# Modulation units summed by VectorE, modulation as columns, and bias masks shared by two engines

## The reference

```
mod = (silu(c) @ w_mod + b_mod)            # 1024 x 6144, one row; block two: w_ada
sh1, sc1, gt1, sh2, sc2, gt2 = split(mod, 6)
h = layer_norm(x) * (1 + sc1) + sh1
y = hybrid_mixer(h, ...)                   # h @ w_in; convolution, state space part, attention, gates, w_o
x = layer_norm(alpha * x + (1 + gt1) * y)
h = layer_norm(x) * (1 + sc2) + sh2
y = hierarchical_moe(h, ...)               # 16 experts
# block two: latent attention, three banded attentions with
#   bias_table[t5_bucket(pos_k - pos_q)] added to the scores, 16 wider experts
```

## Time and profile before

| | us |
|---|---|
| median of 3 runs | 2214.21 (2212.7 to 2215.25) |
| the profiled execution | 2215.75 |
| its span | 2213.9 |
| TensorE busy | 1644.6 (74%) |
| VectorE busy | 440.2 (20%) |
| ScalarE busy | 287.3 (13%) |
| GpSimd busy | 104.3 (5%) |
| DMA | 670.55 MB, 303 GB/s in the mean |
| granted clock of TensorE | 0.873 |

### The profile page before, as it was taken

The page is one execution under the profiler, slowest core; times in us unless marked ns, Lnnn a source line. Parts: engine busy times, 40 slices in busy tenths (PEclk is TensorE's granted clock), DMA queues, the critical chain, the costliest instruction groups (busy, mean ns, idle before and its releaser), DMA issues.

```text
span 2213.9 us, 19952 instructions
## 1 busy us (share of the span) xinstructions
PE 1644.6 (74%) x8097; PEld 860.0 (39%) x8097; DVE 440.2 (20%) x890; ACT 287.3 (13%) x602; POOL 104.3 (5%) x99
## 2 busy tenths in 40 slices
PE   6899999979998699999998744655464544554444
PEld 2575654444443477687754411311121111211111
DVE  6430542342222322121325300000000000000001
ACT  6211222020000222121223100000000000000000
POOL 7000000000000100111111000000000000000000
PEclk9999999979999799999999777877778766877777
DMA  8899444729998342443452479999999999999995
GB/s 276 293 340 341 178 157 142 295 90 429 426 429 316 128 152 78 166 138 133 137 169 105 200 335 428 428 427 429 427 429 427 428 427 428 427 429 427 428 427 247
DMA packets 116171, 670.55 MB, mean 303 GB/s; under 512 B 8643, under 2 KB 11400, under 8 KB 85360
## 3 DMA queue, kind: packets, MB, share of 16 engines
q1 hardware_dynamic: 111568, 657.50, 73.3%
q0 software_dynamic: 3744, 11.11, 1.7%
q10 hardware_dynamic: 768, 0.64, 0.1%
HBM read 661.88 MB, written 7.34 MB: 302 GB/s over the span
## 4 chain that ended last, share of the span: by engine, by line
PE 61%; DMA 31%; DVE 3%; ACT 2%; issue 2%; SPq 1%; POOL 0%; DVEq 0%; ACTq 0%; POOLq 0%
PE psum L914 13%; PE psum L904 12%; DMA ring<-in_w_up 10%; DMA ring<-in_w_down 10%; PE psum L1403 10%; DMA ring<-in_w_gate 9%; PE psum L1217 5%; PE psum L1247 3%; PE psum L872 2%; PE psum L1187 2%; PE psum L1257 1%; PE psum L1143 1%; SPq L643 1%; PE psum L1340 1%; PE psum L1277 1%
## 5 line engine op out<-in xcount | busy, mean ns | idle before, releaser
L1403 PE MATMUL psum<-work,prob 128*32 128x512 f32 x1024 | 286.5, 724 | 159.0 <-DMA ring<-in_w_up 83.9
L1403 PE MATMUL psum<-ring,prob 128*32 128x512 f32 x1024 | 286.5, 724 | 151.1 <-DMA work<-in_w_up 86.2
L914 PE MATMUL psum<-ring,hT 128*128 128x512 f32 x672 | 303.8, 597 | 4.7 <-ACT hT L177 2.9
L904 PE MATMUL psum<-hT,ring 128*128 128x256 f32 x1152 | 277.2, 385 | 1.6 <-DVE hT L177 1.6
L904 PEld LDWEIGHTS psum<-hT,ring 128*128 128x128 f32 x1152 | 213.7, 193 | 36.3 <-issue 10.6
L1403 PE MATMUL psum<-work,hT 128*32 128x512 f32 x512 | 138.4, 703 | 88.8 <-DMA ring<-in_w_down 88.8
L1403 PE MATMUL psum<-ring,hT 128*32 128x512 f32 x512 | 138.4, 703 | 55.6 <-DMA work<-in_w_down 54.0
L914 PEld LDWEIGHTS psum<-ring,hT 128*128 128x128 f32 x672 | 123.9, 191 | 135.7 <-issue 129.1
L1403 PEld LDWEIGHTS psum<-work,prob 128*32 128x32 f32 x1024 | 70.7, 131 | 261.7 <-issue 261.7
L1403 PEld LDWEIGHTS psum<-ring,prob 128*32 128x32 f32 x1024 | 70.6, 131 | 253.1 <-issue 253.1
L177 ACT ACTIVATE work<-psum 128x512 f32<-128x512 f32 (+2 forms) x99 | 56.0, 566 | 608.3 <-PE psum L1389 236.5
(11 more groups left out here) (322 smaller groups left out, 1581.1 us busy)
## 6 DMA issues: line engine op xcount, KB each, us to landing
ring<-in_w_gate SPq DMA_DIRECT2D x40, 2048.0 KB, 19.2
work<-in_w_up SPq DMA_DIRECT2D x40, 2048.0 KB, 20.4
work<-in_w_gate SPq DMA_DIRECT2D x40, 2048.0 KB, 20.4
ring<-in_w_up SPq DMA_DIRECT2D x40, 2048.0 KB, 20.7
ring<-in_w_down SPq DMA_DIRECT2D x40, 2048.0 KB, 19.8
work<-in_w_down SPq DMA_DIRECT2D x40, 2048.0 KB, 20.0
ring<-in_w_in SPq DMA_DIRECT2D x72, 1024.0 KB, 7.4
ring<-in_w_mod SPq DMA_DIRECT2D x24, 1024.0 KB, 8.9
```

What stands on the lines that cost most here:

```text
L904: mm = pe.matmul(o[:, wide(j * S, S)], w[:, ch], actT[:, c, :], start=(c == 0), stop=(c == KC - 1))
L914: mm = pe.matmul(o, actT[:, c, wide(t * P, P)], w, start=(c == 0), stop=(c == KC - 1))
L1403: mm = pe.matmul(o[wide(i * CAP2, CAP2), :], lhs(chunks_per * piece + c, i), R.slot(l + i, (chunks_per, width))[:, c, wide(b * BANK, BANK) ...
```

## The change

1. **Units 2 to 11** are no longer products. `sum_unit(u)` on VectorE multiplies each of eight weight slices (128 x 1024) by a value per partition and adds them up in a 128 x 1024 buffer; `sum_rows(u)` on TensorE then sums over the partitions with two products, whose other operand (`ones_at`) has a column of ones at row u. A unit is now loaded as four loads of two slices with rows of 4 KB, and `read(n)` lets SP wait for VectorE's step as a slot's reader.
2. **Shift and scale 0 and 1** are taken as columns: 16 small products turn `mod_rows` into `mod_cols`, and VectorE and ScalarE scale half of `hT` each. The tokens are only centred and scaled by their deviation before their transposes, which stand ahead of the units.
3. **Positions first**: SP loads positions and x ahead of the table. GpSimd makes no masks; ScalarE takes |position + offset| in four instructions of 128 x 256 for each mask, VectorE compares. Seven mask buffers, four staging buffers of two steps; the copies out are shared by ScalarE and VectorE. The 16 steps are written out among the units and the first chunk; six of them (10 to 15) stand behind that chunk.
4. **Order**: unit u's load and sum take places in the lists by hand; in the attention VectorE makes one multiply-add between two tiles (`between`), in the merges unit 11 is read in two halves.

```diff
+        def read(n):
+            reader = loads[n][2]
+            return reader if isinstance(reader, tuple) else done(reader)
         def load_unit(u):
-            for n in range(2):
-                load_chunk(f"unit{u}_{n}", (w_mod, w_ada)[u // 6], wide(u % 6 * D + n * BANK, BANK), job(f"unit{u}"))
+            src = (w_mod, w_ada)[u // 6].rearrange("(p c) n -> p c n", c=KC)[:, :, wide(u % 6 * D, D)]
+            used = [(unit_used, 3 * u + i + 1) if i < 3 else job(f"unit{u}") for i in range(4)] if u < 2 else [unit_read(u, i) for i in range(4)]
+            unit_loads[u] = [load(src[:, wide(2 * i, 2), :], (2, D), used[i]) for i in range(4)]
...
-                        sp.wait_ge(*done(loads[n - SLOTS][2]))
+                        sp.wait_ge(*read(n - SLOTS))
...
+            fetch_run(16, 18)
+            for g in range(5, BIAS_GROUPS):
+                store_bias(g)
+            fetch_run(18, moe_load0)
...
+            def sum_rows(u):
+                o = begin(job(f"unit{u}"))
+                pe.wait_ge(*unit_read(u, 3))
+                for n in range(2):
+                    mm = pe.matmul(o[wide(64 * n, 64), :], ones_at[:, 31 - u:95 - u], unit_sum(u)[:, wide(n * BANK, BANK)], start=True, stop=True)
+                end(mm)
...
+            def distances(*steps):
+                for s in steps:
+                    if mask_free(s):
+                        act.wait_ge(*mask_free(s))
+                    for q in range(BIAS_QUERIES):
+                        ins = a.activation(one_hot[mask_of[s]][:, q, :], pos_all, ACT.Abs, bias=pos_quarter[:, s * BIAS_QUERIES + q:s * BIAS_QUERIES + q + 1])
+                    ins.then_inc(signal("distance_ready"), 1)
...
+            def sum_unit(u):
+                for c in range(KC):
+                    i, half = divmod(c, 2)
+                    if half == 0:
+                        dve.wait_ge(*arrived(unit_loads[u][i]))
+                    weights, scale = slot(unit_loads[u][i], (2, D))[:, half, :], cact[:, u // 6, c:c + 1]
+                    if c == 0:
+                        step(v.tensor_scalar, unit_sum(u), weights, scale, None, ALU.mult)
+                    else:
+                        step(v.scalar_tensor_tensor, unit_sum(u), weights, scale, unit_sum(u), ALU.mult, ALU.add, signals=unit_read(u, i) if half else None)
+                    yield
...
+                if ct >= 8:
+                    next(unit2)
...
+            whole(sum_unit(3))
+            add_row(2)
+            whole(sum_unit(4))
```

More of the change, by code:

```diff
@@ L15, in build_program @@
     from contextlib import ExitStack
+    from itertools import chain, islice
     from concourse import bass, mybir
@@ L623, in first_free @@
                         last = [next(n for n in range(end - 1, -1, -1) if n % SLOTS == one) for one in (2 * s, 2 * s + 1)]
-                        free.append([done(loads[n][2]) for n in last])
+                        free.append([read(n) for n in last])
                 return free
@@ new lines, in bias_out, with take_hT @@
+            def bias_out(*steps):
+                for s in steps:
+                    stage_free(act, s - 1)
+                    k = job(f"bias{s}", 0)
+                    act.wait_ge(*done(k))
+                    a.activation(staged_half(s, 0), bank(k), ACT.Copy).then_inc(emptied(k)[0], 1)
+            def take_hT(t):
+                for half in range(2):
+                    take(job("hT", 2 * t + half), hT[:, 4 * half:4 * half + 4, wide(t * P, P)], src=lambda o: o.rearrange("p (c t) -> p c t", c=4))
@@ new lines, in _ @@
+            bias_out(1)
+            take_hT(0)
+            distances(4)
+            take_hT(1)
+            distances(5)
+            bias_out(3)
+            distances(6, 7)
+            bias_out(5)
+            distances(8)
+            act.wait_ge(*emptied(job("cols")))
+            for c in range(KC // 2, KC):
+                step(a.activation, hT[:, c, :], hT[:, c, :], ACT.Identity, bias=mod_cols[:, 0, c:c + 1], scale=mod_cols[:, 1, c:c + 1], signals=(signal("hT_high"), c - KC // 2 + 1))
@@ L1749, in normalize, with attention @@
                 step(v.scalar_tensor_tensor, dst[:, t, :], dst[:, t, :], rstd[:, t, 1:2], shift, ALU.mult, ALU.add, signals=signals)
-            def attention(name, n, unit0, masked, keys, out, fills=()):
-                due = {fill_span(f, fills, n)[1]: fill for f, fill in enumerate(fills)}
+            def attention(name, n, unit0, masked, keys, out, between=iter(())):
                 for i in range(n + LAG_PV):
@@ L1773, in _ @@
+            step(v.tensor_copy, pos_all, pos_rows)
             dve.wait_ge(signal("const_in"), 16)
[L1774 to L1781 removed]
@@ new lines, in whole @@
+            def whole(steps):
+                for _ in steps:
+                    pass
+            add_row(0)
+            in_bucket(5)
+            bias_out(3)
+            in_bucket(6)
+            bias_out(4)
+            in_bucket(7)
+            bias_out(5)
+            in_bucket(8)
+            bias_out(6)
+            add_row(1)
+            bias_out(7)
+            k = job("cols")
+            dve.wait_ge(*done(k))
+            by_unit = bank(k)[:, 0:2 * KC].rearrange("p (c u) -> p u c", u=2)
```

407 lines of the change are left out of this document (243 added, 164 removed).

## The result

The change takes 11.2 us off: 2203.4 us in the median of five runs (2199.55 to 2206.8) for 2214.6 (2212.7 to 2215.5) run beside them, a ratio of 0.9947, 95% interval 0.9936 to 0.9958. Forecast were 2188 us, and 26.4 us of gain in the profiled execution. That execution took 2201.38, so it gained 14.4. The range (2169 to 2207) holds the time, but the gain was little more than half of the forecast in the profiled execution, and less than half in the medians.

What follows compares the result with a forecast made beforehand. Expert stages, with DMA 94 to 97% busy, stay untouched; the first 411 us, bias masks then gapless TensorE, are at stake. 31.4 - 1.6 + 9 - 12.4 = 26.4 us gained: 2188 us in the median, eight in ten 2169 to 2207.

Steps and rivals of the forecast that it cites:

- its clock: First input projection chunk: it ran cold before, 16.69 us against 14.01; half of that stays, gain 1.4 us.
- six masks behind it: Behind the first projection chunk: 12 mask products of 0.9 us on TensorE, cost 10.8 us, not below 10.
- units less pairs: Input projection: eight units of 3.57 us go, five summing pairs cost 4.5 us; net gain 24.1 us.
- The start: Before the first projection chunk: cheaper masks and normalising ahead of modulation bring it to 44 us from 74.7, gain 30.7.
- The ring: Projection: slots wait for VectorE's reads, delaying q's loads; TensorE waits about 11 us, then loses 3; cost 14.
- The attention: First attention: unit pieces of 11.8 us go, VectorE's multiply-adds between tiles cost 3; gain 9 us, bounds 2 and 12.
- VectorE catches up in the filled tiles: First attention: eight tiles have a fill and let VectorE catch up; multiply-adds cost between 0 and 10 us, taken as 3.
- The merges: Merges: unit 11's late load makes TensorE wait 7.5 us; with pairs 3.6 and clock 1.3, cost 12.4, bounds 4 and 18.
- A: Rival: q waits 4 us, unit 11 waits 2, attention gains 12; 2172 to 2174 us; chance 0.18.
- B: Rival: projection loads land 12 us after issue instead of 7, four stages lose 5 each; 2208 us; chance 0.09.
- C: Rival: DMA writes to the ring slow VectorE's multiply-adds to 2.4 us a step; 2221 us; chance 0.08.
- D: Rival: each of seven TensorE waits costs the full 2.7 us of low clock; 2203 us; chance 0.08.

Runs made afterwards that it cites:

- mask 9 early: Changed kernel with mask 9's subtractions ahead of ScalarE's four scalings and its comparison ahead of VectorE's second modulation row: 2198.7 us, ratio 0.9926.
- The weights-first order: Changed kernel with the loads of q, k, v and two z chunks each ahead of the modulation unit's four loads: 2191.9 us, ratio 0.9908.
- The short multiply-adds: Changed kernel with VectorE's multiply-adds on unit weights cut to 16 of 1024 columns, leaving out most of the sums: 2190.8 us, ratio 0.9893.
- the changed kernel's second profile: Profile from running the changed kernel again, unchanged: median 2206.5 us, ratio 0.9968.
- the best kernel here: Changed kernel with weights first, unit 11 late, masks 9 and 0 early, attention multiply-adds paired in filled tiles, GpSimd's small loads after x: 2170.1 us, ratio 0.9801.
- the two best: The best kernel here (2170.1 us) and the same without the later small loads (2170.9 us, ratio 0.9802).
- the third: Changed kernel with only one edit: attention multiply-adds two at a time in the eight tiles with a fill, none in the others: 2202.0 us, ratio 0.9947.

## Why the prediction was right and wrong

| Term | forecast | profiled |
|---|---|---|
| first chunk earlier | +30.7 | +23.7 |
| its clock | +1.4 | +2.2 |
| six masks behind it | -10.8 | -11.0 |
| units less pairs | +24.1 | +23.4 |
| ring | -14 | -12.5 |
| at the cumulative sum (the mark) | 31.4 | 24.3 |
| from there to the first merge | +5.6 | +3.3 |
| merges | -10.6 | -12.9 |
| to the first expert product | 26.4 | 14.4 |

(The pairs of units 8 and 9 run ahead of the first merge and stand in that line, not in the one of the merges. The lines ahead of the mark leave 1.5 us open, 0.6 of it in q's chunk. Behind the last merge 0.3 more is lost.) Of the 12.0 us that the gain fell short, 7.1 arose ahead of the mark, 2.3 from there to the first merge, 2.3 in the merges.

**The start** is the step that failed most: the first chunk was forecast at 44 and came at 51.0, 7.0 us late, the largest part of the miss. Step by step: the first two masks were forecast done at 14 us and ended at 19.0. x landed 3.8 later than in the earlier trace rows, and their four products took 6.3 us where the forecast took 0.9 each, 3.6. (They look like products at the low clock, but the profile gives a granted clock of 1.00 there, so this cause is not shown.) Units, transposes and six masks then took 21.5, not 23. The tail was forecast at 7 and took 10.5. Its own terms (2, four times 0.42, 1.7 + 0.75 and 1.8) already make 7.9, and the copies, given no price, took 0.4. A ScalarE scaling takes 0.60, not the 0.42 of the earlier trace rows, which has no column operand where this has two. And the last mask's products, priced at 1.8, took 3.0 behind the wait that the forecast itself had put into the chain (granted clock 0.63 from 48 to 51 us). That wait was not needed: with mask 9 early 4.5 us come back. The 1.7 for a mask's four subtractions came out right by luck: with one column operand each they take 0.50 and not 0.42, but overlap, so that four in a row take 1.69.
The Trainium skill (ScalarE: Activation LUTs, What ACT_TABLE_LOAD costs) says that each per-partition pointer operand, such as a column of scales, adds some 93 ns to an ACTIVATE. By that rule a scaling costs 0.19 more than the row; measured is 0.18 more, so the trace agrees.

**The ring** was right in mechanism and size: 9.75 us for 11 at q, ended by the load, then 2.7 in three waits for 3. The weights-first order shows that it is an order. The short multiply-adds show that VectorE's own time moves q's start by 2.2 us, near the 2.6 that the forecast had for it, and no more.

**The attention** gained less than forecast: multiply-adds and their gaps cost 4.6 us in the profiled run, where 3 was the value and 10 the bound (the units' 11.8, less 2.7 for the two pairs, which ran at a low clock, less the 4.4 that were gained between the first score and the first merge). What failed is the step "VectorE catches up in the filled tiles, so TensorE's waits are all that is lost". They are not: in some runs the clock falls behind them, 5.4 us more in the changed kernel's second profile, and the forecast counted no clock here. The medians of the changed kernel lie 2 and 5 us above its first profiled run, in which the clock stayed; that this is why is likely, but the other runs have no profile.

**The merges** lost what was forecast, by the mechanism that was forecast: wait 9.0 for 7.5, and the pair of unit 11 at 2.0 behind it for 0.9. Here no step fell; the sum was 2.3 short, 1.5 of it the wait.

**Rivals.** A (the ring hides more): no. B (the loop through VectorE doesn't fit): no, waits of 0.6 to 1.5 at v and z. C (multiply-adds slowed by the DMA's writes): no, 1.285 us. D (the full 2.7 of clock at each of seven waits) came to about the right time, but not by its mechanism. Behind the waits of 0.6 to 1.5 us at v and z the chunks ran at full clock, 13.97 us. Behind the wait for the late mask and the one in the merges the clock was low for a while (0.63 from 48 to 51 us, 0.66 from 384 to 388). At q the chunk behind the 9.75 us wait took 15.9, 1.9 over the 14.0 of the earlier trace rows, but this is not the price of the wait: with the weights first there was no wait and it took 15.95, and before the change, with no wait, 15.3. What stands ahead of q in all three is the small products of `dtf`, 24 columns each, and the clock falls while TensorE works on them or just behind (windows before, changed, weights first):

```profile
151.00:153.00 2.00, 2.00 (x13) 1.91 (x13) 0.47 (x3) 0.00 (x0) 0.00 (x0) 0.68 1.05 390
```

```profile
120.00:122.00 2.00, 2.00 (x12) 1.93 (x11) 1.86 (x3) 0.00 (x0) 0.00 (x0) 0.61 0.84 309
```

```profile
120.00:122.00 2.00, 2.00 (x13) 1.93 (x12) 1.86 (x3) 0.00 (x0) 0.00 (x0) 0.71 0.83 285
```

TensorE is busy for the whole of each window. The largest clock loss that the forecast had left out, in the attention, is at none of D's waits.
The rule it rested on in the Trainium skill (TensorE: Matmul & The Clock Gate, HAM oscillation) speaks of waits for DMA in each turn of a loop; here such waits of 0.6 to 1.5 us, shorter than those of its example, left the clock alone, and in the attention it fell behind gaps ended by other engines.

**Open.** Two profiles of one kernel had the same waits in the attention, and in one the clock fell; what decides was not found. Why the first four mask products take 5.4 to 6.7 us is not shown either. Nor what x shares the DMA engines with: the constants, at 506 KB issued in the same microsecond and landed after 6.1, and the ring's loads behind x were not moved.

## What to carry to other kernels

When a second engine starts to read what a shared ring holds, its reads become part of the load queue: give the loads the order of need, and put whatever only sums for later behind, which was worth 22 of the 44 us that the best kernel here gains. A product that waits for a side result should be placed where its engine idles anyway; what is queued behind the wait is the price, not the product. And where small products wait on VectorE tile by tile, count its extra work twice: the gap costs once, and the clock after it may cost again, in some runs and not in others. Spreading the work so that the gaps stay short is worth a trial; here it took away the worst profiles and not every fall.

## What was not expected of the hardware

- With the same code and the same waits, the granted clock in one stretch of some 60 us was 0.99 in one execution and 0.90 in the next, worth 5.4 us. With TensorE busy 4.2 of 5 us in the attention's middle gaps it fell in one place alone, the same in three kernels, and the runs of the two best agreed within 0.4 and 1.9 us, those of the third within 4.4.
- The clock fell with TensorE busy for the whole window, at products of 24 columns: 0.68 from 151 to 153 us before the change. The chunk behind took 15.3 to 15.95 us, with and without a wait ahead of it, for 14.0.
- ScalarE's 128x256 instruction took 0.60 us with two column operands, 0.50 with one (mean of 56 mask subtractions) and 0.42 with none; four mask subtractions in a row overlap and took 1.69 together.
- x, the same 1 MB, landed 5.0 us after its issue in one program and 8.8 in the other; holding 16 small loads back made it 8.4.
